# The triangular inverse of a chunked RWKV-7 scan: five levels on 32x32 blocks, the sixth as one block per head

## The reference, cut to what matters

```python
def rwkv_scan(r, w, k, v, kk, a, s0, reverse):
    def step(S, xs):
        r_t, w_t, k_t, v_t, kk_t, a_t = xs
        sa = jnp.einsum("bhvk,bhk->bhv", S, kk_t)
        S = (S * w_t[:, :, None, :] - sa[..., None] * (kk_t * a_t)[:, :, None, :]
             + v_t[..., None] * k_t[:, :, None, :])
        return S, jnp.einsum("bhvk,bhk->bhv", S, r_t)
    xs = tuple(jnp.swapaxes(t, 0, 1) for t in (r, w, k, v, kk, a))
    s_fin, ys = lax.scan(step, s0.astype(jnp.float32), xs, reverse=reverse)
    return jnp.swapaxes(ys, 0, 1), s_fin
```

## Time and profile before

| | |
|---|---|
| median of 3 runs | 1624.02 us (1620.69 to 1624.89) |
| the profiled execution, span | 1626.1 us |
| TensorE matmul busy | 1471.8 us (91%), 10008 instructions |
| TensorE weight loads | 709.2 us (44%), 10009 |
| VectorE | 524.1 us (32%), 976 |
| ScalarE | 262.0 us (16%), 514 |
| GpSimd | 100.1 us (6%), 191 |
| moved by DMA | 510.78 MB, of it 0.82 MB in 50 packets of an instruction queue (q8) |

### The profile page before, as it was taken

One profiled execution on the slowest core, in us unless ns is written; L12 is line 12 of the kernel. 1 busy time (PEld: TensorE's weight loads), 2 busy tenths in 40 slices (PEclk: granted clock), 3 DMA queues, 4 the chain that ended last, 5 costly groups with the idle time before them and its releaser, 6 DMA issues.

```text
span 1626.1 us, 26117 instructions
## 1 busy us (share of the span) xinstructions
PE 1471.8 (91%) x10008; PEld 709.2 (44%) x10009; DVE 524.1 (32%) x976; ACT 262.0 (16%) x514; POOL 100.1 (6%) x191
## 2 busy tenths in 40 slices
PE   4899998988997977999989999999999998998994
PEld 1677666767783452333323333333332332332331
DVE  2564544777777652101101101101011011110126
ACT  0332333221300210101101101101111010110110
POOL 1000000000001000000000000000000000000021
PEclk8899998999897977999999999999999999999996
DMA  9556835000016486999999999999999999999995
GB/s 363 201 191 238 324 133 187 2 9 3 2 55 218 148 353 278 420 421 421 422 421 421 422 421 421 422 421 422 422 420 422 421 421 421 420 422 422 421 406 189
DMA packets 97928, 510.78 MB, mean 314 GB/s; under 512 B 14752, under 2 KB 17072, under 8 KB 45160
## 3 DMA queue, kind: packets, MB, share of 16 engines
q1 hardware_dynamic: 82680, 480.08, 72.7%
q10 hardware_dynamic: 10336, 17.18, 2.8%
q0 software_dynamic: 4848, 12.59, 2.1%
HBM read 491.03 MB, written 22.71 MB: 316 GB/s over the span
## 4 chain that ended last, share of the span: by engine, by line
PE 64%; DMA 15%; DVE 10%; SPq 7%; issue 3%; ACT 1%; POOL 0%; DVEq 0%; ACTq 0%; POOLq 0%
PE bank L718 51%; PE bank L722 10%; SPq L595 6%; DMA ring<-w_moe_in 5%; DMA work<-w_moe_in 3%; DMA spare<-w_moe_in 3%; PE bank L725 3%; DVE work L2052 1%; DMA zbuf<-w_ada 1%; DMA work<-rows_d,dest 1%; DVE work L1781 1%; DVE work L1760 1%; DVE work L2053 1%; DVE work L1784 1%; ACT work L1235 1%
## 5 line engine op out<-in xcount | busy, mean ns | idle before, releaser
L718 PE MATMUL bank<-work 64*64 64x64 f32 (+3 forms) x5134 | 534.0, 355 | 39.0 <-DMA work<-w_moe_in 9.6
L718 PEld LDWEIGHTS bank<-work 64*64 64x64 f32 (+2 forms) x5134 | 246.4, 137 | 289.4 <-issue 235.8
L718 PE MATMUL bank<-ring,work 128*64 128x512 f32 (+1 forms) x1376 | 352.4, 606 | 17.0 <-DMA ring<-w_moe_in 10.9
L2046 DVE TENSOR_SCALAR work<-bank 128x512 f32<-128x512 f32 x39 | 27.0, 692 | 752.1 <-PE bank L718 752.1
L718 PEld LDWEIGHTS bank<-ring,work 128*64 128x64 f32 (+1 forms) x1376 | 115.4, 145 | 224.8 <-issue 192.8
L1235 ACT ACTIVATE work<-bank 128x512 f32<-128x512 f32 (+2 forms) x223 | 110.6, 513 | 561.5 <-PE bank L718 323.1
L722 PE MATMUL bank<-parts 128*128 128x512 f32 (+1 forms) x720 | 167.1, 386 | 3.0 <-DVE parts L448 3.0
L718 PE MATMUL bank<-zbuf,work 64*64 64x64 f32 (+2 forms) x966 | 139.1, 387 | 12.7 <-DMA zbuf<-w_moe_in 4.7
L722 PEld LDWEIGHTS bank<-parts 128*128 128x128 f32 x720 | 128.5, 190 | 33.6 <-issue 5.2
L1462 ACT ACTIVATE work<-work 128x512 f32<-128x512 f32 x39 | 24.6, 630 | 468.9 <-DVE work L2046 468.9
L718 PEld LDWEIGHTS bank<-zbuf,work 64*64 64x64 f32 (+2 forms) x966 | 65.2, 141 | 76.3 <-issue 58.5
(11 more groups left out here) (264 smaller groups left out, 862.6 us busy)
## 6 DMA issues: line engine op xcount, KB each, us to landing
work<-w_moe_in SPq DMA_DIRECT2D x108, 1024.0 KB, 22.8
ring<-w_moe_in SPq DMA_DIRECT2D x84, 1024.0 KB, 25.6
work<-w_moe_out SPq DMA_DIRECT2D x64, 1024.0 KB
ring<-w_moe_out SPq DMA_DIRECT2D x44, 1024.0 KB, 22.1
ring<-w_ada SPq DMA_DIRECT2D x11, 2048.0 KB, 7.7
zbuf<-w_moe_in SPq DMA_DIRECT2D x22, 1024.0 KB, 26.7
first<-w_moe_in SPq DMA_DIRECT2D x21, 1024.0 KB
spare<-w_moe_in SPq DMA_DIRECT2D x21, 1024.0 KB
```

The costliest lines, as they stand in the source:

```text
L718: return pe.matmul(out, l, r, start=start, stop=stop)
L2046: ts(gl, B[0], LIMIT, None, ALU.min).then_inc(S["thd"], 1)
```

## The change

A doubling level below 32 only mixes tokens within blocks of 32. Levels 0 to 4 now run on the 32x32 diagonal blocks alone: four blocks a head (two chunks, two halves), one for each quarter of the partitions, so that a row of all heads has 8 x 32 = 256 columns instead of 512. `eighths` does such a product: 8 heads by 4 quarters, 32 products of 32x32 by 32x32 on the four diagonal 32x32 tiles of TensorE. The running inverse is XC (in 32 columns a head), its transpose XM. The level-0 part needs the diagonal blocks of the Gram matrix with all quarters in the same columns; `diagonal_gram` makes these anew on TensorE (32 products a direction, after the first two AM copies have freed the banks). Level 5 is one 32x32 block per head and chunk: `across` does 16 products. VectorE expands XC to the 64-column XT with zeros elsewhere, and ScalarE copies PM of level 5 and puts the new block into XT with its sign turned. BON waits for level 5's second product, since it lies in the place of XC. Some semaphores are merged (tcA and tcV to tcs, lnld to stld).

```diff
+QB = HC // 2
+SMALL = LEVELS - 1
@@ masks, in 32 columns
+    sq, cq = s % QB, np.arange(QB)[None, :]
     for d in range(2):
-        for l in range(LEVELS):
+        for l in range(SMALL):
...
-    lev.append(sm == ch)
+    lev.append(sq == cq)
+    lev += [np.broadcast_to(sm // QB == i, (P, QB)) for i in range(2)]
@@ buffers
-        XM, XT = two(3072, HR, HC), two(3584, HR, HC)
+        XC, XM, XT = two(3072, HR, QB), two(3328, HR, QB), two(3584, HR, HC)
-        PM, GM, UV, UU = (two(6144 + i * DR, HR, HC) for i in range(4))
+        PM, S0D = two(6144, HR, QB), two(6400, 4, HD)
+        GM, UV, UU = (two(6656 + i * DR, HR, HC) for i in range(3))
-        NP, NX = LEVELS - 1, 2 * LEVELS - 1
+        NP, NX = LEVELS - 1, 2 * SMALL + 3
@@ TensorE
+            part = lambda q: slice(QB * q, QB * (q + 1))
+            def diagonal_gram(d):
+                for c in range(4):
+                    for par in range(2):
+                        r = rows_of(par)
+                        for q in range(4):
+                            last = mm(bk(d, 2 * par)[part(q), part(c)], BKT[d][r, 0, c, part(q)], QRT[d][r, c, 0, part(q)])
+                return last
+            def eighths(bank, l, r):
+                for h in range(HR):
+                    for q in range(4):
+                        last = mm(bank[part(q), part(h)], l(q, h), r[part(q), h, :])
+                return last
+            def across(bank, d, l, r, into):
+                for h in range(HR):
+                    for b in range(2):
+                        src, dst = 2 * b + (d if into else 1 - d), 2 * b + (1 - d if into else d)
+                        last = mm(bank[part(dst), part(h)], l(src, dst, h), r[part(src), h, :])
+                return last
...
                 for d, j in pair:
+                    pe.wait_ge(S["am"], 4 * (2 * p + d) + 2)
+                    diagonal_gram(d).then_inc(S["gdiag"], 1)
+                for d, j in pair:
                     pe.wait_ge(S["am"], 4 * (2 * p + d) + 4)
                     quads(bank_block(bk(d, 3)), blocks(AM[d], 2), values_of(j)).then_inc(s_u[d], 1)
...
-                        quads(bank_block(bk(d, 0)), blocks(AM[d], 0), blocks(XM[d])).then_inc(s_p[d], 1)
+                        if l <= SMALL - 1:
+                            ins = eighths(bk(d, 0), lambda q, h: AM[d][part(q), h, 0, part(q % 2)], XM[d])
+                        else:
+                            ins = across(bk(d, 0), d, lambda src, dst, h: AM[d][part(src), h, 0, part(dst % 2)], XM[d], True)
+                        ins.then_inc(s_p[d], 1)
...
-                        quads(bank_block(bk(d, 2)), blocks(PM[d]), blocks(XT[d])).then_inc(s_d[d], 1)
+                        if l <= SMALL - 1:
+                            ins = eighths(bk(d, 2), lambda q, h: PM[d][part(q), h, :], XC[d])
+                        else:
+                            ins = across(bk(d, 2), d, lambda src, dst, h: PM[d][part(src), h, :], XC[d], False)
+                        ins.then_inc(s_d[d], 1)
@@ ScalarE, ahead of its copies of WT
+                for d, j in pair:
+                    sc.wait_ge(s_p[d], NP * p + SMALL)
+                    sc.wait_ge(s_d[d], NP * p + SMALL - 1)
+                    cp(flat(PM[d]), bk(d, 0)[:, 0:HR * QB]).then_inc(s_pc[d], 1)
+                for d, j in pair:
+                    sc.wait_ge(s_d[d], NP * p + SMALL)
+                    sc.wait_ge(s_x[d], NX * p + 2 * SMALL + 1)
+                    for b in range(2):
+                        r = slice(QB * (2 * b + d), QB * (2 * b + d + 1))
+                        cp(XT[d][r, :, QB * (1 - d):QB * (2 - d)], bk(d, 2)[r, 0:HR * QB].rearrange("p (h t) -> p h t", h=HR), -1.0)\
+                            .then_inc(s_x[d], 1)
@@ VectorE
-                    ve.wait_ge(S["am"], 4 * (2 * p + d) + 4)
-                    L(tt(XT[d], AM[d][:, :, 0, :], transposed, M))
-                    tt(XT[d], idb, XT[d], SUB).then_inc(s_x[d], 1)
+                    ve.wait_ge(S["gdiag"], 2 * p + d + 1)
+                    by_pair = XC[d].rearrange("p (c q) t -> p c q t", q=2)
+                    both(*[tt(by_pair[:, :, par, :], bk(d, 2 * par)[:, 0:4 * QB].rearrange("p (c t) -> p c t", c=4),
+                              transposed, M) for par in range(2)])
+                    tt(XC[d], idb, XC[d], SUB).then_inc(s_x[d], 1)
...
-                for l in range(1, LEVELS):
+                for l in range(1, SMALL):
...
-                        tt(XT[d], XT[d], by_head(bk(d, 2)), SUB).then_inc(s_x[d], 1)
-                        if l < LEVELS - 1:
-                            ve.wait_ge(s_x[d], NX * p + 2 * l + 1)
-                            ve.transpose(flat(XM[d]), flat(XT[d])).then_inc(s_x[d], 1)
+                        tt(XC[d], XC[d], by_head(bk(d, 2)), SUB).then_inc(s_x[d], 1)
+                        ve.wait_ge(s_x[d], NX * p + 2 * l + 1)
+                        ve.transpose(flat(XM[d]), flat(XC[d])).then_inc(s_x[d], 1)
+                for d, j in pair:
+                    halves_of = XT[d].rearrange("p h (i t) -> p h i t", i=2)
+                    own_half = levelm[:, 2 * SMALL + 1:2 * SMALL + 3, :].unsqueeze(1).broadcast_to([P, HR, 2, QB])
+                    tt(halves_of, XC[d].unsqueeze(2).broadcast_to([P, HR, 2, QB]), own_half, M).then_inc(s_x[d], 1)
+                for d in range(2):
+                    ve.wait_ge(s_x[d], NX * p + 2 * SMALL + 1)
+                    ve.wait_ge(s_d[d], NP * p + SMALL)
                 both(*[tt(BON[d], KD[d], zr[d], M) for d in range(2)])
```

More of the change, by code:

```diff
@@ L131, in constants @@
     lev = []
+    sq, cq = s % QB, np.arange(QB)[None, :]
     for d in range(2):
-        for l in range(LEVELS):
-            same = (sm >> (l + 1)) == (ch >> (l + 1))
-            tb, sb = (sm >> l) & 1, (ch >> l) & 1
+        for l in range(SMALL):
+            same = (sq >> (l + 1)) == (cq >> (l + 1))
+            tb, sb = (sq >> l) & 1, (cq >> l) & 1
             lev.append(same & ((sb == 0) & (tb == 1) if d == 0 else (sb == 1) & (tb == 0)))
-    lev.append(sm == ch)
+    lev.append(sq == cq)
+    lev += [np.broadcast_to(sm // QB == i, (P, QB)) for i in range(2)]
     out["c_level"] = np.concatenate(lev, 1).astype(np.uint16) * np.uint16(0x3F80)
@@ L178, in build @@
         gram16 = sb("gram16", [P, 2 * 4 * HC], U16)
-        level16 = sb("level16", [P, (2 * LEVELS + 1) * HC], U16)
+        level16 = sb("level16", [P, (2 * SMALL + 3) * QB], U16)
         gramm = gram16[:, :].bitcast(BF16).rearrange("p (d n) -> p d n", d=2)
-        levelm = level16[:, :].bitcast(BF16).rearrange("p (l n) -> p l n", n=HC)
+        levelm = level16[:, :].bitcast(BF16).rearrange("p (l n) -> p l n", n=QB)
         rope = sb("rope", [P, 2, 2, 2, 16])
@@ L351, in build @@
         names = """adald cond modld n1 xld modd ssq rstd htok htr hTa hTv wdone zmm zA zV cons2 cons3
-        cachekv stored aqk kdupd qtr ktr qTa kTv smm nmax prob rinv ptr ptc pv ya tg ttr tcA
-        tcV kkss kkr stld sttr stev lora lt1 ltanh lw lcum lexp rqd bkd ttr4 rqT wsm s0p gram am yout
-        yrd twod st2 sftr sfcp sfout lnld gld gps yfin ytr yTc upm upad mga mrg mtr mTc wout g1l x1s
+        cachekv stored aqk kdupd qtr ktr qTa kTv smm nmax prob rinv ptr ptc pv ya tg ttr tcs kkss kkr stld sttr stev lora lt1 ltanh lw lcum lexp rqd bkd ttr4 rqT wsm s0p gram am yout
+        yrd twod st2 sftr sfcp sfout gld gps yfin ytr yTc upm upad mga mrg mtr mTc wout g1l x1s
         h2out h2tr h2Tc lg tabled summed sqd b32 b3d cmpd idxm idxc xgd xtm xtc gmm mult hi thd actd atm atc
-        yc yo fin chain uud rsc gpn zfill chain2v modrow condq routeq""".split()
+        yc yo fin chain uud rsc gpn zfill chain2v modrow condq routeq gdiag""".split()
         S = {n: sem("s_" + n) for n in names}
@@ L556, in _ @@
             for dst, src in ((lnw, "rw_ln_w"), (lnb, "rw_ln_b")):
-                sp.dma_start(dst, a[src].broadcast_to([P, DR])).then_inc(S["lnld"], 16)
+                sp.dma_start(dst, a[src].broadcast_to([P, DR])).then_inc(S["stld"], 16)
             sp.dma_start(gld[0], gates_d[0]).then_inc(S["gld"], 16)
@@ L867, in _ @@
                 last.then_inc(S["sttr"], 1)
-            pe.wait_ge(S["tcA"], 2)
-            pe.wait_ge(S["tcV"], 1)
+            pe.wait_ge(S["tcs"], 3)
             pe.wait_ge(S["stev"], 2)
@@ L1323, in _ @@
                 sc.wait_ge(S["ttr"], i + 1)
-                cp(dst, B[i][:, 0:NT * P]).then_inc(S["tcA"], 1)
+                cp(dst, B[i][:, 0:NT * P]).then_inc(S["tcs"], 1)
             flat = lambda v: v.rearrange("p a b -> p (a b)")
@@ L1700, in _ @@
             ve.wait_ge(S["ttr"], 2)
-            cp(adT, B[1][:, 0:NT * P]).then_inc(S["tcV"], 1)
+            cp(adT, B[1][:, 0:NT * P]).then_inc(S["tcs"], 1)
             for d in range(2):
@@ L1706, in _ @@
             ve.wait_ge(S["modd"], 16 * ADG)
-            idb = levelm[:, 2 * LEVELS:2 * LEVELS + 1, :].broadcast_to([P, HR, HC])
-            by_head = lambda bank: bank.rearrange("p (h t) -> p h t", h=HR)
```

(6 more changed lines are left out.)

2 lines of the change are left out of this document (1 added, 1 removed).

## The result

The changed kernel takes 1656.51 us (median of 4 runs, 1654.41 to 1659.49), the kernel before 1622.82 (4 runs, 1620.69 to 1624.89): a ratio of 1.021, 95% interval 1.0189 to 1.0231, so 31 to 37 us slower by the interval. The profiled executions differ by 27.3 us (spans 1653.4 and 1626.1).

What follows compares the result with a forecast made beforehand. In the changed inversion, instruction fetch was to bind, 3.65 us per 256 instructions: 3 x (7.5 + 0.5) - 0.9 + 4 = +27 us, 1653 profiled, 1651 as median. Own range 1638 to 1668; 8 in 10, 1622 to 1673.

Steps and rivals of the forecast that it cites:

- A: Rival: instruction fetch keeps up and the inversion's loop with VectorE binds; 1599 us, or 1611 with 58 ns; 9 in 100.
- B: Rival: TensorE's queue running ahead hides the next fetch's start, a block costs some 2.65 us; 1622 us; 7 in 100.
- D: Rival: the four row tiles of eighths write one bank and exclude each other; 1665 to 1740 us; 2 in 100.
- C: Rival: as forecast, but the low clock stays over the whole scan behind the inversion; 1680 us; 5 in 100.
- (1) to (3): Levels 1 to 4, level 5, then WT and UV: 2560 instructions at the fetch's pace, +7.5 us a pair (6.2 to 9.0).
- What the loop would be without the fetch: Level period of levels 1 to 4 if only TensorE and VectorE bound it: 3.07 us, against 4.93 before.
- The bound with 58 ns: Level period without the fetch if 32 columns gain nothing, four tiles' matmuls taking 58 ns: 3.97 us.
- (4): diagonal_gram ahead of GM: 256 instructions in all, mostly taken by TensorE's idle time; +0.5 us a pair (0.1 to 1.9).
- (5): First pair's VectorE bonus operations, formerly last, now lie beside ScalarE's copies before TensorE is done: -0.9 us, once.
- (7): Granted clock falls after rests in the block-bound stretch, slowing the products behind the inversion: 4 us in all (0 to 9).

Runs made afterwards that it cites:

- Run 1: Kernel before with each level product cut into two halves of 32 weight columns, 512 instructions a level instead of 256: 1662.76 us, ratio 1.0227.
- run 2: Changed kernel with levels 1 to 4 in half the instructions, odd heads multiplied with their neighbour's weights (computes something else, for time alone): 1613.65 us, ratio 0.9934.
- block-diagonal form: Another form of the change: levels 1 to 4 with 64x64 block-diagonal weights, 256 instructions a level: 1621.66 us, 0.9992 of the kernel before; with w_out transfer moved, 1621.75.
- run 128: Not a follow-up run: a verb and a count, 32x32 weights on four tiles run 128 matmuls and their loads in 1.93 us.

## Why the prediction was right

**The mechanism held.** The forecast was 1651 us, the median 1656.5; for the profiled execution 1653, and it came to 1653.4. Rivals A and B are out: packets lie 3.6 to 3.9 us apart on average, none near 2.65. D is out: 128 matmuls of 32x32 took 1.93 us, 15 ns each, so four row tiles, each in its own quarter of the partitions, write one bank side by side. C is out in its form: the granted clock was 1.00 behind the second inversion. The instruction queue brought 15 packets more, the number forecast. Run 1 shows that the count of instructions alone makes such a loss, run 2 that taking it away gives the time back.

The rule weighed there (the Trainium skill, "Runtime: NRT & Kernel Launch", Instruction fetch mechanics: the fetch is hidden behind dispatch) does not hold for these products, by the stops of 1.6 to 2.1 us. Nor does the Trainium skill's "TensorEngine Tiling (Array Packing)", Gotcha 1: PSUM Pressure, that row tiles can't use one bank at once, hold for these tiles, by the 15 ns.

**Its terms, one by one**, by the profiled executions:
- (1) to (3), from level 1 to UV: +7.5 us a pair forecast (6.2 to 9.0), +10.3, +8.5 and +11.4 measured, 7.7 more in all. The block time was mis-sized. I took 3.65 us from the two borders seen before; it was 3.9 in the first pair and 3.6 in the second. In the second pair, then, the 1.0 us too much is not the block time: there the last block before the copy of UV took 4.9 us (420.69 to 425.56, at a mean clock of 0.58), where the sum ended with half a block in 0.9. The third pair had its late packet on top. Two of three pairs fell outside the bounds.
- What the loop would be without the fetch: 3.07 us forecast, 2.9 measured (run 2, with 64 columns on four tiles). The bound with 58 ns is a slip: its parts add up to 3.85 us, not 3.97, which moves the second time of rival A by about 1 us and the forecast not at all.
- (4) the front: +0.5 (0.1 to 1.9) forecast, +0.7, +0.5 and +1.6 measured.
- (5) the bonus term: -0.9 forecast. Half of it came and was lost again: VectorE's last operation of the first pair starts 14.8 us behind the start of the copy of UV, and 15.3 before, but the transposes that follow (8 matmuls) fell under the low clock (1.89 us, and 1.24 before). To the next pair's first LoRA products it is 18.2 us, and was 18.1.
- (7) the clock: +4 us forecast, and this step failed. The low clock did not come after the inversion but over it, 0.59 to 0.61 in the mean. There it cost little: in run 1, at 0.96 and 1.00, a block is shorter by 0.15 us at most, an estimated 1.5 us a pair. And it was over when the dense products came, which in the second pair gave 3.4 us back.

So the inversions and fronts lost 33 us where 24 were forecast, and the stretches between them gave 6 back where 3 more were to be lost. That the sum met the profile within 1 us is luck: two errors against each other. The medians are 33.7 us apart, 6 more than the two profiled executions. The span of before lies 3.3 us over the median of that kernel, the changed one's 3.1 us under its own, and runs of before spread over 15 us (1618.51 to 1633.5).

**What stays open.** Why a block takes anything from 3.6 to 3.9 us. The changed kernel has 3.9 in pair 1 and 3.6 in pair 2, run 1 has 3.8 and 3.6 at nearly the full clock, and run 2 has 3.7 in pair 1. And whether the block-diagonal form would beat the kernel before if the transfer were issued behind the small loads of the norm: no run did that.

## What to carry to other kernels

Count instructions before columns. In these kernels, once the blocks fetched ahead were used up, 256 instructions of TensorE (loads of weights counted) cost 3.6 to 3.9 us however little they did, so splitting a product into smaller tiles paid only as long as the stretch stayed above that. A stop by "issue" inside a run of like instructions, with packets of the instruction queue at even distances, is the sign. Two such stops, of 0.42 and 0.56 us in the kernel before, were enough to foresee the limit. To use a structure in the data without more instructions, pack it into larger weights (block-diagonal): here that took 3.1 us off the undisturbed first pair, but no shorter time of the whole is shown. Keep large transfers away from stretches that live from one packet to the next, and don't put them ahead of small loads that the next stage waits for.

## What the runs showed of the hardware

- A transfer of 2 MB under a block-bound stretch holds back the next instruction packet: a stop of 4.9 us with it and 1.9 without in the changed kernel, 1.5 us with it and none without in the block-diagonal form.
- The same transfer of 2 MB, issued 1 us ahead of two loads of 256 KB, kept VectorE waiting 3.9 us for the second of them, in three kernels alike (3.88, 3.89, 3.91).
- What the low clock costs depends on what binds. At 0.5 the block-diagonal level went from 4.04 to 6.83 us, while the changed kernel's blocks took 3.9 us at 0.59 and run 1's 3.8 at 0.96.
- 32x32 weights on four tiles run 128 matmuls and their loads in 1.93 us at the low clock (15 ns each); 64x64 weights with 32 columns need 31 ns (544 in 16.86 us, without a stop by "issue"), no less than with 64 columns (128 in 4.02). Halving the columns of a 64x64 tile bought TensorE nothing here.
